# A two-block transformer kernel: one of four depthwise-convolution channel blocks moved to GpSimd, weight sums and output adds re-placed

## The reference, cut to what matters

```python
def first_block(x, ...):
    h = rmsnorm(x, g_mix)
    a_in, q, k, v, f_logit, gate_a, gate_b = jnp.split(h @ w_in, COL_SPLITS, axis=-1)
    a = a_in[..., :512] * sigmoid(a_in[..., 512:])          # the gated linear unit, 512 channels
    a = causal_depthwise_conv(a, w_dw, b_dw)                # 31 taps, one filter per channel
    a = silu(layernorm(a, g_conv_ln, b_conv_ln)); y_conv = a @ w_conv_out
    y_attn = forgetting_attention(q, k, v, f_logit, ...) @ w_attn_out   # 8 heads of 64
    x = x + (sigmoid(gate_a) * y_conv + sigmoid(gate_b) * y_attn) @ w_out
    gu = rmsnorm(x, g_ffn) @ w_ffn_in
    return x + (silu(gu[..., :2816]) * gu[..., 2816:]) @ w_ffn_out

def second_block(h, ...):
    ...                                                     # mixer: differential attention and a short convolution
    xn = modulate(rmsnorm(h), sh2, sc2)
    ff = ec_moe(xn, w_router, w_gate, w_up, w_down)         # 16 experts, 128 tokens each
    return h + g2 * rmsnorm(ff, norm_post_ffn)
```

## Time and profile before

| | |
|---|---|
| median of 3 runs | 2755.16 us (2754.34 to 2761.09) |
| the profiled execution | 2763.52 us, its span 2762.3 us |
| busy share of the span | PE 96%, DVE 67%, ACT 46%, POOL 18% |
| mean granted TensorE clock | 0.98 |
| chain of waits that ended last | PE 22%, DVE 3% of the span |
| tail behind the last matmul | 2736.2 to 2762.3 us |

### The profile page before, as it was taken

One profiled execution on the slowest core, in us unless ns is written; L12 is line 12 of the kernel. 1 busy time (PEld: TensorE's weight loads), 2 busy tenths in 40 slices (PEclk: granted clock), 3 DMA queues, 4 the chain that ended last, 5 costly groups with the idle time before them and its releaser, 6 DMA issues. The chain is left out here.

```text
span 2762.3 us, 35670 instructions
## 1 busy us (share of the span) xinstructions
PE 2641.3 (96%) x13421; PEld 2212.3 (80%) x13421; DVE 1842.2 (67%) x2259; ACT 1274.0 (46%) x1918; POOL 485.6 (18%) x661
## 2 busy tenths in 40 slices
PE   8999999999999999999999999989998599999995
PEld 7788888788898877777888898878877588888884
DVE  4277776652427888886556433389845788888887
ACT  4144344241225333333445312188733377777775
POOL 4323220000003222222011220012232300000102
PEclk9999999999999999999999999999998799999998
DMA  8321120111313445566764532001234699999996
GB/s 276 126 70 47 53 66 16 46 54 46 117 55 118 138 150 170 176 206 223 245 191 156 149 74 68 13 20 29 72 131 168 226 379 393 394 395 395 396 395 245
DMA packets 249513, 461.88 MB, mean 167 GB/s; under 512 B 16588, under 2 KB 138176, under 8 KB 247936
## 3 DMA queue, kind: packets, MB, share of 16 engines
q1 hardware_dynamic: 219520, 354.83, 36.5%
q0 software_dynamic: 29712, 104.75, 11.3%
q10 hardware_dynamic: 112, 0.03, 0.0%
HBM read 384.79 MB, written 65.32 MB: 163 GB/s over the span
## 5 line engine op out<-in xcount | busy, mean ns | idle before, releaser
L502 PE MATMUL ps<-r,r 128*128 128x512 f32 (+2 forms) x10316 | 2271.4, 378 | 18.7 <-DVE r L487 5.5
L502 PEld LDWEIGHTS ps<-r,r 128*128 128x128 f32 x10316 | 1848.2, 189 | 368.6 <-DVE r L487 12.9
L479 ACT ACTIVATE r<-f 128x2048 fp32r<-128x2048 f32 (+2 forms) x339 | 504.1, 1493 | 401.9 <-PE ps L502 393.2
L3698 DVE TENSOR_TENSOR r<-f,r 128x2048 fp32r<-128x2048 f32 x188 | 429.1, 2291 | 63.9 <-ACT r L479 62.7
L487 DVE TENSOR_TENSOR r<-f,r 128x1024 fp32r<-128x1024 f32 (+1 forms) x151 | 168.9, 1131 | 330.0 <-ACT r L479 329.8
L502 PE MATMUL ps<-f,f 128*128 128x64 f32 (+3 forms) x1410 | 219.8, 305 | 1.9 <-ACT f L1250 1.6
L502 PEld LDWEIGHTS ps<-f,f 128*128 128x128 f32 (+1 forms) x1410 | 180.8, 193 | 24.8 <-issue 21.2
L872 DVE SCALAR_TENSOR_TENSOR f<-f,misc,f 128x1023 f32<-128x1023 f32 (+29 forms) x120 | 154.2, 1312 | 0.0
L1977 ACT ACTIVATE r<-f 128x512 fp32r<-128x512 f32 x140 | 87.1, 629 | 72.1 <-PE ps L502 57.7
L1166 ACT ACTIVATE f<-ps,misc 128x128 f32<-128x128 f32 (+7 forms) x64 | 47.5, 743 | 146.0 <-DVE misc L1155 146.0
L3716 POOL DMA_INDIRECT ff_scratch<-f,misc x15 | 28.8, 1917 | 474.5 <-ACT f L3827 412.2
(11 more groups left out here) (342 smaller groups left out, 2193.9 us busy)
## 6 DMA issues: line engine op xcount, KB each, us to landing
f<-in_w_gate_dram SPq DMA_DIRECT2D x64, 1024.0 KB, 8.4
f<-in_w_up_dram SPq DMA_DIRECT2D x64, 1024.0 KB, 10.2
f<-in_w_down_dram SPq DMA_DIRECT2D x64, 1024.0 KB, 8.0
f<-in_w_in_dram SPq DMA_DIRECT2D x56, 512.0 KB, 4.5
f<-in_w_ada_dram SPq DMA_DIRECT2D x96, 256.0 KB, 4.8
f<-in_w_ffn_in_dram SPq DMA_DIRECT2D x80, 256.0 KB, 4.1
hid_scratch<-f POOLq DMA_DIRECT2D x77, 256.0 KB, 2.8
f<-hid_scratch SPq DMA_DIRECT2D x35, 512.0 KB, 5.4
```

Of the source, the lines that this page charges most:

```text
L479: self.act.activation(hi, raw, ACT.Copy).then_inc(self.sem(st.name + "_hi"), 1)
L502: return self.pe.matmul(o, left, right, start=start, stop=stop, skip_group_check=True)
L3698: self.dve.tensor_tensor(es.lo[i % 4], es.raw[i % 8], es.hi[i % 4].bitcast(F32), ALU.subtract).then_inc(self.sem("e_lo"), 1)
```

## The change

Four things are changed together.

1. DVE makes the taps of three channel blocks (93). POOL makes those of the fourth, one tap behind each tile of `pool_project`: a `tensor_scalar` of `CA` into a scratch tile `tap`, then a `tensor_tensor` that adds it to `CO`. `TAPS` drops from 3 to 2 in the steps with 3.
2. All 11 sets of weight sums are made in `pool_front`, in three buffers, and none between the attention's tiles.
3. Piece 8 (the forget columns) stands in place 5 and not in place 2. Place 2 is the first block's whole 1024 columns, place 5 its second half; piece 9, the first of the attention, stands in the first half (place 4).
4. At the end the residual x is stored straight into the output by `pool_wout2` and not into a scratch. For tiles 0 to 3 DVE leaves out the addition, and POOL adds the tile into the output with an accumulating DMA. The last expert's row is made behind tile 7 and not behind tile 4.

```diff
@@ -56,4 +56,4 @@
     (("n1_hat", 8), ("pj_ms", 32)),
-    (("w_lo", 143), ("a2_fac", 96), ("n4_ms", 8), ("hid", 32), ("out_dve", 8)),
-    (("n1_lo", 16), ("glu", 8), ("fg_two", 1), ("fg_d", 11), ("taps", 124), ("ln_add", 6), ("ln_ms", 2),
+    (("w_lo", 143), ("a2_fac", 96), ("n4_ms", 8), ("hid", 32), ("out_dve", 4)),
+    (("n1_lo", 16), ("glu", 8), ("fg_two", 1), ("fg_d", 11), ("taps", 93), ("ln_add", 6), ("ln_ms", 2),
      ("mg_add", 16), ("n2_ss", 2), ("ada", 16), ("n3_ss", 2), ("n3_lo", 16), ("rp_sign", 2), ("rp_sin", 8),
@@ -179,2 +179,3 @@
         self.x_in = a["x"].rearrange("o s d -> (o s) d")
+        self.out_rows = self.out.rearrange("o s d -> (o s) d")
@@ -198,3 +199,3 @@
         self.HT = self.pair(0, 32, 8, 1024)
-        self.CA, self.CO = f(121, 4, 1024), f(137, 4, 1024)
+        self.CA, self.CO, self.tap = f(121, 4, 1024), f(137, 4, 1024), f(193, 1024)
         self.fgT = f(105, 1024)
@@ -433,3 +434,3 @@
-        slot = [i % 3 for i in range(self.i_pj)]
+        slot = [i % 3 for i in range(self.i_pj - 1)] + [5]
         slot += [4 + 2 * q + h for _ in range(4) for h in range(2) for q in range(3)]
@@ -557,11 +558,10 @@
         pool.wait_ge(*sem("n1_T", 1))
-        for j in range(2):
-            self.pool_sums_load(self.SUM_SETS[j][0], j)
-        for n in range(3):
-            for j in range(2):
-                self.pool_sums_make(self.SUM_SETS[j][n], j, (0, 1, 2, 3))
-                if n < 2:
-                    self.pool_sums_load(self.SUM_SETS[j][n + 1], j)
+        for m in range(3):
+            self.pool_sums_load(m, m)
+        for m in range(11):
+            self.pool_sums_make(m, m % 3)
+            if 3 <= m + 2 < 11:
+                self.pool_sums_load(m + 2, (m + 2) % 3)
-    SUM_SETS = (0, 2, 4), (1, 3, 5), (6, 7, 8, 9, 10)
+    SUM_SETS = (0, 3, 6, 9), (1, 4, 7, 10), (2, 5, 8)
@@ -587,5 +587,4 @@
             pool.tensor_tensor(out, x, y, ALU.subtract).then_inc(sem("t_sum"), 1)
-        if steps[-1] == 3:
-            pool.wait_ge(*sem("t_sum", 4 * m + 4))
-            pool.dma_start(self.ffo_dram[m * P:(m + 1) * P, :], self.out_raw[j]).then_inc(sem(f"t_out{j}"), 16)
+        pool.wait_ge(*sem("t_sum", 4 * m + 4))
+        pool.dma_start(self.ffo_dram[m * P:(m + 1) * P, :], self.out_raw[j]).then_inc(sem(f"t_out{j}"), 16)
@@ -859,4 +858,4 @@
         dve, sem = self.dve, self.sem
-        for k in range(self.taps, min(self.taps + n, 124)):
-            tap, ct = k // 4, k % 4
+        for k in range(self.taps, min(self.taps + n, 93)):
+            tap, ct = k // 3, k % 3
             wc = self.colsB[:, (30 - tap) * 4 + ct:(30 - tap) * 4 + ct + 1]
@@ -866,3 +865,3 @@
                 for j in range(2):
-                    dve.wait_ge(*sem(f"t_out{j}", 48))
+                    dve.wait_ge(*sem(f"t_out{j}", 64))
                 dve.tensor_scalar(self.CO[:, ct, :], self.CA[:, ct, :], wc, self.col("b_dw", ct), ALU.mult,
@@ -870,3 +869,3 @@
             else:
-                dve.wait_ge(*sem("taps", k - 3))
+                dve.wait_ge(*sem("taps", k - 2))
                 dve.scalar_tensor_tensor(out=self.CO[:, ct, tap:], in0=self.CA[:, ct, 0:S - tap], scalar=wc,
@@ -874,3 +873,22 @@
                     sem("taps"), 1)
-        self.taps = min(self.taps + n, 124)
+        self.taps = min(self.taps + n, 93)
+
+    def pool_taps(self, n):
+        pool, sem = self.pool, self.sem
+        c = self.CO[:, 3, :]
+        for k in range(self.taps_pool, min(self.taps_pool + n, 31)):
+            wc = self.colsB[:, (30 - k) * 4 + 3:(30 - k) * 4 + 4]
+            if k == 0:
+                pool.wait_ge(*sem("glu", 8))
+                pool.wait_ge(*sem("cols", 3))
+                for j in range(3):
+                    pool.wait_ge(*sem(f"t_out{j}", (64, 64, 48)[j]))
+                pool.tensor_scalar(c, self.CA[:, 3, :], wc, self.col("b_dw", 3), ALU.mult, ALU.add).then_inc(
+                    sem("taps_p"), 1)
+            else:
+                pool.wait_ge(*sem("taps_p", k))
+                pool.tensor_scalar(self.tap[:, k:], self.CA[:, 3, 0:S - k], wc, None, ALU.mult).then_inc(sem("tap_p"), 1)
+                pool.wait_ge(*sem("tap_p", k))
+                pool.tensor_tensor(c[:, k:], c[:, k:], self.tap[:, k:], ALU.add).then_inc(sem("taps_p"), 1)
+        self.taps_pool = min(self.taps_pool + n, 31)
@@ -963,3 +981,4 @@
                 if s == 63:
-                    self.act.wait_ge(*self.sem("t_out2", 80))
+                    self.act.wait_ge(*self.sem("t_out2", 48))
+                    self.act.wait_ge(*self.sem("taps_p", 31))
                 self.high(self.ws, min(self.i_pj + 6 * (s // 16 + 1) + 3, self.i_ga + 1))
@@ -989,3 +1008,3 @@
-    TAPS = (3, 3, 2, 3, 1, 1, 1, 1, 1, 1, 1, 1, 2, 3, 1, 1)
+    TAPS = (2, 2, 2, 2, 1, 1, 1, 1, 1, 1, 1, 1, 2, 2, 1, 1)
@@ -1102,6 +1121,3 @@
             pool.tensor_copy(self.QK[j][:, 2:4, 64:65], heads(self.ncc)).then_inc(sem("pj_aug"), 1)
-            if n % 5 == 1 and n < 25:
-                self.pool_sums_load(6 + n // 5, 2)
-            elif n % 5 in (3, 4) and n < 25:
-                self.pool_sums_make(6 + n // 5, 2, ((0, 1), (2, 3))[n % 5 - 3])
+            self.pool_taps(1)
@@ -1342,6 +1358,7 @@
             self.low(self.ws, self.i_ga + mt + 3)
-            self.dve_taps(124)
+            self.dve_taps(4 if mt < 2 else 93)
             if mt == 3:
-                dve.wait_ge(*sem("taps", 124))
+                dve.wait_ge(*sem("taps", 93))
+                dve.wait_ge(*sem("taps_p", 31))
                 for c in range(2):
@@ -3351,3 +3368,3 @@
                 sem(f"dma_xh{i % 3}"), 16)
-            pool.dma_start(self.x3_dram[i * P:(i + 1) * P, :], self.Xt[i]).then_inc(sem("dma_x4"), 16)
+            pool.dma_start(self.out_rows[i * P:(i + 1) * P, :], self.Xt[i]).then_inc(sem("dma_x4"), 16)
@@ -3725,3 +3742,3 @@
         pool.wait_ge(*sem("dma_x4", 16 * NT))
-        for dst, rows, name in ((self.XS, self.ff_dram, "dma_lf"), (self.last_x, self.x3_dram, "dma_lx")):
+        for dst, rows, name in ((self.XS, self.ff_dram, "dma_lf"), (self.last_x, self.out_rows, "dma_lx")):
             pool.indirect_dma_start(
@@ -3938,5 +3955,6 @@
+    ONTO = 4
+
     def sp_out(self):
         sp, sem = self.sp, self.sem
-        out = self.out.rearrange("o s d -> (o s) d")
         sp.wait_ge(*sem("scat", 16 * (NE - 1)))
@@ -3945,6 +3963,8 @@
             sp.dma_start(self.F[i], self.ff_dram[i * P:(i + 1) * P, :]).then_inc(sem(f"x{i}"), 16)
-        for i in range(NT):
-            sp.wait_ge(*sem("out_dve", i + 1))
-            sp.dma_start(out[i * P:(i + 1) * P, :], self.F[i]).then_inc(sem("out"), 16)
-        sp.wait_ge(*sem("out", 16 * NT))
+        sp.wait_ge(*sem("dma_lx", 16))
+        for i in range(self.ONTO, NT):
+            sp.wait_ge(*sem("out_dve", i - self.ONTO + 1))
+            sp.dma_start(self.out_rows[i * P:(i + 1) * P, :], self.F[i]).then_inc(sem("out"), 16)
+        sp.wait_ge(*sem("out_sum", 16 * self.ONTO))
+        sp.wait_ge(*sem("out", 16 * (NT - self.ONTO)))
         sp.wait_ge(*sem("dma_last", 16))
@@ -3970,11 +3990,17 @@
         for i in range(NT):
-            if i == 5:
-                pool.wait_ge(*sem("last_ms", 1))
-                pool.tensor_tensor(self.mst[0][:, 1:2], self.mst[0][:, 0:1], self.nhalf[:, 0:1], ALU.pow).then_inc(
-                    sem("last_inv"), 1)
             self.pool_inverse("n5", i, i + 1, i + 1)
+            if i == 2:
+                pool.wait_ge(*sem("dma_lx", 16))
+            if 2 <= i < self.ONTO + 2:
+                pool.wait_ge(*sem("n5_hat", i - 1))
+                pool.dma_start(self.out_rows[(i - 2) * P:(i - 1) * P, :], self.F[i - 2], accum_op=ALU.add).then_inc(
+                    sem("out_sum"), 16)
+        pool.wait_ge(*sem("last_ms", 1))
+        pool.tensor_tensor(self.mst[0][:, 1:2], self.mst[0][:, 0:1], self.nhalf[:, 0:1], ALU.pow).then_inc(
+            sem("last_inv"), 1)
         pool.wait_ge(*sem("last_row", 1))
-        pool.wait_ge(*sem("out", 16 * NT))
+        pool.wait_ge(*sem("out_sum", 16 * self.ONTO))
+        pool.wait_ge(*sem("out", 16 * (NT - self.ONTO)))
         pool.indirect_dma_start(
-            self.out.rearrange("o s d -> (o s) d"), bass.IndirectOffsetOnAxis(ap=self.iT[:, NE - 1:NE], axis=0), self.XS,
+            self.out_rows, bass.IndirectOffsetOnAxis(ap=self.iT[:, NE - 1:NE], axis=0), self.XS,
             None, bounds_check=S - 1).then_inc(sem("dma_last"), 16)
@@ -3983,9 +4009,10 @@
         dve, sem = self.dve, self.sem
-        dve.wait_ge(*sem("n5_sq", 1))
-        self.dve_mean("n5", 0, 1)
+        for i in range(2):
+            dve.wait_ge(*sem("n5_sq", i + 1))
+            self.dve_mean("n5", i, i + 1)
         dve.wait_ge(*sem("dma_g2", 16))
         for i in range(NT):
-            if i + 1 < NT:
-                dve.wait_ge(*sem("n5_sq", i + 2))
-                self.dve_mean("n5", i + 1, i + 2)
+            if i + 2 < NT:
+                dve.wait_ge(*sem("n5_sq", i + 3))
```

(13 more changed lines are left out.)

6 lines of the change are left out of this document (3 added, 3 removed).

## The result

The changed kernel is slower: median 2766.65 us (8 runs, 2761.88 to 2768.77) against 2757.69 us for the kernel before in the same series (8 runs); the ratio is 1.003, 95% interval 1.0019 to 1.0041. The forecast was 2733 us. The two profiled executions differ by 5.2 us of span (2767.5 against 2762.3). Along the program the difference is, from their timelines: 5.5 us earlier at the first power of the attention, 19.0 us later at the last one, 13.5 later at the convolution's sum, 9.3 later at the last 36 matmuls, 5.2 later at the scatter. So the loss lies between the first and the last power of the attention (a power is POOL's -0.5 power in a tile's norm, one for each of the 32 tiles), and most other terms have about the size that was forecast.

What follows compares the result with a forecast made beforehand. TensorE (PE) was taken to be busy nearly everywhere, so only ending its waits pays. Terms -7 - 4 - 6.9 - 1 + 1 - 5 sum to -22.9 us; from 2755.2 that is 2732.3, stated as 2733 us, range 2725 to 2748.

Steps and rivals of the forecast that it cites:

- E: Attention: the fourth block's taps on POOL, 6.3 us a tile, just fit between powers; +1 us (0 to +11.5).
- D: Attention: 31 taps (39 us) leave DVE, partly offset by contention with GpSimd; -1 us (-3 to +3).
- rival 5: Attention: multiplication costs 4.9 us, POOL's tile 9.5, powers late; slower, 2776 us, deciding from 8.6 us a tile; chance 0.07.
- rival 3: Attention: POOL paces the short tiles mildly at 7.65 us each, with two clock dips; 2744 us, chance 0.12.
- A: Start of attention: with piece 8 moved, PE's wait goes and the forget gates' sum comes earlier; -7.0 us (-4.4 to -7.5).
- Rival 1: Front: weight sums come late, DVE's first tap waits until about 132, gain there only -1; 2739 us, chance 0.10.
- B: Middle of attention: without transfers between tiles, weight pieces land earlier, ending a PE wait and clock dip; -4 us (0 to -5).
- C: Behind the attention: no 13 taps left on DVE, so PE's gate products run without waiting; -6.9 us (-4.6 to -6.9).
- F: Tail: DVE drops four additions, last expert's row moves, last store leaves earlier; -5 us (-7.4 to -3.0, 0 at worst).
- rival 2: Tail: the accumulating DMAs take the whole gain there; 2738 us, chance 0.12.

Runs made afterwards that it cites:

- experiment 11: Changed kernel with POOL's addition ahead of its multiplication and the multiplication in two-operation form (mult, add 0.0); ratio 0.9958 to the kernel before.
- experiment 17: Changed kernel without VectorE's taps after its first three, GpSimd's taps whole (three of four blocks not computed); 2730.37 us.
- experiment 4: Changed kernel with GpSimd making only an addition of the shifted block, no multiplication (fourth block not the convolution); 2737.7 us.
- experiment 13: Changed kernel with GpSimd's addition cut to 16 columns in the ten long tiles (6, 7 and 8 of a group); 2744.72 us.
- experiment 14: Changed kernel with GpSimd's addition cut to 16 columns in the other 20 tiles, whole in the ten long ones; 2761.19 us.
- experiment 8: Changed kernel with all 124 taps on VectorE and the last 13 spread over later steps behind the attention; 2735.64 us.
- experiment 9: As experiment 1 (all taps on VectorE), but with piece 8 in place 2 again; ratio 0.9971 to the kernel before.
- experiment 1: Changed kernel with all four blocks (124 taps) back on VectorE, the rest of the change kept; 2741.62 us.
- experiment 10: As experiment 1, but with the output and tail as before the change; ratio 0.9968 to the kernel before.
- experiment 2: Changed kernel without GpSimd's taps, VectorE keeping its 93 (fourth block not computed); 2738.48 us.
- experiment 7: Changed kernel with GpSimd's multiplication in two-operation form (mult by the column, add 0.0); 2753.86 us.
- experiment 15: Changed kernel with one VectorE tap, not two, in the first and third step of a group; 2758.40 us.
- experiment 5: Changed kernel with GpSimd's two instructions in turned order, adding the previous tile's product first, then multiplying for the next tap; 2747.60 us.
- experiment 3: Changed kernel with GpSimd making only each tap's multiplication, no addition (fourth block not summed); 2737.7 us.
- experiment 6: Changed kernel with GpSimd's addition replaced by a second multiplication (fourth block not computed); 2750.22 us.

## Why the prediction was wrong

**E and D failed**, and with them the sign. E bounded the taps on POOL by POOL's own queue: so many us a tile against so many between powers, "it just fits". For the powers that was right, even though the multiplication took 2.83 us and not 1.7: the tile was 6.6 us, below the 8.6 from which rival 5 was to decide, and experiments 11 and 17 show that the queue cost the powers next to nothing. Both signs that the prediction had named for its being wrong came (gaps of 8.3 us between the first powers, PE's waits behind the exponential at 14.0 us and not 3.8), but not from POOL's queue, on which rivals 3 and 5 put the loss. The price was paid by the other engine. The row that mattered was in the prediction (a tap of 2370 ns beside a GpSimd subtraction), but it was booked as a sum of lost VectorE time against a sum of relief (D: -1, at worst +3). By experiment 4 that sum, 24 us, can be free; by experiments 13 and 14 the additions of ten tiles cost 22 us. What had to be asked was, for each place of the addition, what VectorE does there and how much room it has before its next maximum: 0.26 us. E also left out a wait that the change itself adds: ACT's for GpSimd's last tap. In numbers: E was +1 and came out at 26.9 us of attention (341.8 - 314.9). Of these, 18.8 lie in nine long gaps, where additions hold up VectorE's work before a maximum; 3.2 lie in the tenth, where ACT waits for the last tap; and 4.9 lie in the short gaps. The 18.8 have in them some 1.8 us of a clock of 0.50 behind such a wait. D was -1: the relief was 0 in the long gaps, and 3.0 us were lost in the first steps, through a count of taps that mixes kinds of 0.8 and 1.26 us.

The Trainium skill's rule in "SBUF — State Buffer", Who interferes with whom, was cited for this and weighed at +3 for D; the trace bears the rule out for the addition (a tap of 3.48 us beside an addition of 2.38) and not the weight that I gave it. The same section of the Trainium skill calls the shared ports an exclusive lock. The multiplication does not fit that: a tap that began 0.2 us behind one (146.82 and 146.62 us, changed kernel) took 1.99 us and ended 0.7 us before the multiplication did. The Trainium skill's "GPSIMD Engine Reference", Engine selection, advises to leave two-input elementwise work to VectorE; experiment 8, some 31 us faster than the changed kernel by the ratios, agrees with it. Its one-input rate is near the two-operation form (1.1 us for 1023 elements) and far from the one-operation form (2.83 us).

**A held**, somewhat smaller: -7.0 forecast, 5.5 by the timelines of experiment 9. Rival 1 did not come: the last front store was issued at 121.67 (about 121 forecast). **B held**: -4 forecast, 5.2 in the long gaps of experiment 1 (4.4 of them in the two gaps from 267.66 to 297.96 us, in which the forecast had its rows); in the changed kernel it is hidden below E. **C held**: -6.9 forecast, 34.4 - 27.3 = 7.1 measured. It was tied to the move to GpSimd in the prediction; experiment 8 has it without. **F held**: -5 forecast, 4.1 between the two profiles, 6 to 7 by experiment 10; rival 2 came only in part: VectorE is done 6.3 us earlier, and 2.3 us of that are lost again because the last store lands later. POOL spent 0.85 to 1.02 us on the issue of each accumulating DMA. Without D and E the forecast was -22.9; experiment 8, which is A, B, C and F, gives -23. That it agrees so well is partly luck, since A came out smaller than forecast and B and F (by experiment 10) larger.

On the profiles the terms close: -5.5 (A) + 24.5 (attention: E 26.9, D 2.9, B -5.3) - 7.0 (C) - 4.1 (F) is +7.9, against +5.2. Of the rest, 1.6 us were added between the last power and the gates: the clock reads 0.82 from 470 to 475 us there, behind PE's wait of 3.12 us, and in experiment 2, where PE has no such wait, 1.00. The other 4.3 us came back between the convolution and the tail, in stages that the change doesn't touch. That part is not explained: the profiled execution of before had a mean clock of 0.98 there (540 to 2700 us), that of the changed kernel 0.99.

Two sums of the prediction are slightly off and change nothing: A's 41.99 + 80 is 122 and not 121 (POOL's last front store came at 121.67), and rival 5's 9.5 us a tile give an excess of some 25 us by the earlier trace rows and not 26. The 7.65 us a tile of rival 3 stand without a working.

## What to carry to other kernels

Work put on an idle engine is not paid only in that engine's queue: look at what the other engine runs at the same moment, and at the room it has before the next thing that someone waits for. A sum of stretched instructions says little; two orders of the same two instructions were 18 us of attention apart here. Count the new waits too: one that ACT got for the last tap stood in the path once. And when a change joins parts, ask of each gain if it needs the part it is bound to: here the end of the attention was to be had by spreading 13 taps.

## What had not been expected of the hardware

- GpSimd's `tensor_scalar` of 128 x 1023 with a column of scalars took 2.83 us (median of 30) with one operation and 1.11 us with mult and add 0.0. The difference was there without VectorE's taps too (2.83 us in experiment 17).
- Both engines are held. A VectorE tap of 1.26 us took up to 3.48 us beside an addition of 2.38; the addition took up to 3.15 us (3.23 in experiment 7, 3.46 in experiment 15) where it met taps, the one-operation multiplication up to 4.21 us in experiment 5.
- A tap that began just behind a one-operation multiplication took 1.6 to 2.0 us (experiment 3; at most 2.13 in experiment 6): less than beside an addition, but not nothing.
